# Two neighbouring rows per partition in the expert gate and up weight loads of an encoder trunk, one core

## The reference, cut to what matters

```python
def grouped_moe(h, w_router, router_bias, w_gate, w_up, w_down):
    t = h.reshape(-1, dm)                       # 512 tokens x 1024 in the kernel
    ...                                         # scores, a group of 4 experts, top 2 in it
    out = jnp.zeros_like(t)
    for e in range(N_EXPERTS):                  # 16
        a = jax.nn.silu(t @ w_gate[e]) * (t @ w_up[e])     # (1024, 512) each
        out = out + gate[:, e:e + 1] * (a @ w_down[e])     # (512, 1024)
    return out
```

## Time and profile before

| | |
|---|---|
| median of three runs | 1633.03 us (1631.05 to 1634.56) |
| profiled execution, its own time | 1634.32 us |
| its span, first to last instruction | 1632.7 us |
| TensorE matmul busy | 1432.0 us, 88% |
| VectorE busy | 1010.3 us, 62% |
| ScalarE busy | 874.8 us, 54% |
| granted TensorE clock, mean | 0.951 of full speed |
| bytes moved by DMA | 342.29 MB |

### The profile page before, as it was taken

How to read it: one execution, slowest core, us unless ns; L and a number is a source line. 1 busy time by engine, 2 the same in 40 slices (tenths; PEclk the granted TensorE clock), 3 DMA queues, 4 the chain that set the end, 5 groups by cost and what they waited for, 6 DMA issues and landing times.

```text
span 1632.7 us, 19147 instructions
## 1 busy us (share of the span) xinstructions
PE 1432.0 (88%) x6710; PEld 1083.7 (66%) x6710; DVE 1010.3 (62%) x1258; ACT 874.8 (54%) x1242; POOL 134.6 (8%) x145
## 2 busy tenths in 40 slices
PE   6799989999749999999769989899995699999996
PEld 3577558887537777777537765687772577777774
DVE  1464674324567888888372938633446688878875
ACT  4532585223237777777363328832323577777764
POOL 1000000000010222222000000000000112222210
PEclk9899999999869999999889999999997799999998
DMA  9532571112257999999762136311322799999954
GB/s 331 187 108 98 207 256 54 52 52 103 103 209 268 367 347 334 346 346 340 268 234 103 52 134 245 138 52 53 108 99 103 281 333 349 338 349 345 344 190 159
DMA packets 148654, 342.29 MB, mean 210 GB/s; under 512 B 8430, under 2 KB 10624, under 8 KB 148464
## 3 DMA queue, kind: packets, MB, share of 16 engines
q1 hardware_dynamic: 136880, 317.20, 53.9%
q0 software_dynamic: 10992, 23.43, 3.9%
q10 hardware_dynamic: 720, 0.84, 0.2%
HBM read 334.10 MB, written 24.12 MB: 219 GB/s over the span
## 4 chain that ended last, share of the span: by engine, by line
PE 56%; DMA 15%; DVE 10%; issue 8%; ACT 8%; POOLq 2%; DVEq 0%; PEldq 0%; SPq 0%; ACTq 0%; PEld 0%
PE bank L725 11%; PE bank L727 11%; PE bank L726 11%; DMA y_by_choice<-zone,row_now 7%; DMA zone<-rows_by_token,row_now 5%; PE bank L1068 2%; PE bank L1070 2%; PE bank L1069 2%; DVE w_lo L2149 2%; PE bank L758 2%; POOLq L2282 2%; PE bank L1053 2%; PE bank L1054 2%; PE bank L1055 1%; ACT x_lo L1456 1%
## 5 line engine op out<-in xcount | busy, mean ns | idle before, releaser
L725 PE MATMUL bank<-x_hi,w_lo 128*128 128x512 f32 x608 | 246.0, 405 | 28.1 <-DVE x_lo L1661 17.4
L727 PE MATMUL bank<-x_hi,w_hi 128*128 128x512 f32 x608 | 239.1, 393 | 0.0
L726 PE MATMUL bank<-x_lo,w_hi 128*128 128x512 f32 x608 | 238.7, 393 | 0.0
L2149 DVE TENSOR_TENSOR w_lo<-ring,zone_r 128x2048 fp32r<-128x2048 f32 x92 | 210.4, 2290 | 27.7 <-ACT zone_r L1456 27.7
L1456 ACT CAST x_lo<-ring 128x2048 fp32r<-128x2048 f32 x96 | 184.1, 1920 | 62.6 <-PE bank L1055 26.2
L1456 ACT CAST zone_r<-ring 128x2048 fp32r<-128x2048 f32 x96 | 183.0, 1914 | 24.0 <-PE bank L1070 13.9
L1638 DVE TENSOR_TENSOR w_lo<-ring,w_hi 128x1024 fp32r<-128x1024 f32 x84 | 102.4, 1221 | 98.7 <-ACT w_hi L1211 98.3
L1053 PE MATMUL bank<-w_lo,zone_r 128*128 128x512 f32 x384 | 157.4, 410 | 5.8 <-issue 5.8
L725 PEld LDWEIGHTS bank<-x_hi,w_lo 128*128 128x128 f32 x608 | 114.9, 189 | 65.2 <-issue 26.1
L726 PEld LDWEIGHTS bank<-x_lo,w_hi 128*128 128x128 f32 x608 | 115.4, 190 | 25.4 <-issue 2.4
L727 PEld LDWEIGHTS bank<-x_hi,w_hi 128*128 128x128 f32 x608 | 115.2, 189 | 25.0
(11 more groups left out here) (296 smaller groups left out, 2704.4 us busy)
## 6 DMA issues: line engine op xcount, KB each, us to landing
ring<-in_w_gate SPq DMA_DIRECT2D x32, 2048.0 KB
ring<-in_w_up SPq DMA_DIRECT2D x32, 2048.0 KB, 13.7
ring<-in_w_down SPq DMA_DIRECT2D x32, 2048.0 KB, 8.7
ring<-in_w_ada SPq DMA_DIRECT2D x24, 2048.0 KB, 9.0
ring<-in_w_in SPq DMA_DIRECT2D x16, 2048.0 KB, 8.4
ring<-in_w_out SPq DMA_DIRECT2D x4, 2048.0 KB, 7.8
zone<-y_by_choice SPq DMA_DIRECT2D x8, 1024.0 KB, 8.1
ring<-in_w_branch_a SPq DMA_DIRECT2D x2, 2048.0 KB, 8.4
```

Of the source, the lines that this page charges most:

```text
L725: mm(out, lo, x_first, start=start, stop=False)
L726: mm(out, hi, x_second, start=False, stop=False)
L727: return mm(out, hi, x_first, start=False, stop=stop)
L2149: v.tensor_tensor(w_low[EXPERT_SLOTS[par][k]][:, cols], ring[EXPERT_SLOTS[par][k]][:, cols], part_hi[buf].bitcast(F32), ALU.subtract)\
```

## The change

The gate and up loads read `128 x 4 x 1024` instead of `128 x 8 x 512`: the partition `p` of block `b` takes the two neighbouring weight rows `256b + 2p` and `256b + 2p + 1`, one piece of 4096 bytes. Chunk `c = 2b + j` of a slot now holds rows `256b + 2p + j`. To match, ScalarE's copy of the transposed token rows sets the columns apart: it reads every second element of a PSUM bank and writes runs of 128, so that block `c` of a gathered row holds the same features. The down loads keep their form, written in the same expression.

```diff
@@ first tile's weights of a layer (SyncE)
                 for k, (name, s) in enumerate(zip(("w_gate", "w_up", "w_down"), EXPERT_SLOTS[0])):
                     sp.wait_ge(used[s], layer * SLOT_BLOCKS[s] + SLOT_BLOCKS[s])
-                    sp.dma_start(ring[s][:, :].rearrange("p (k n) -> p k n", k=(KC, KC, FC)[k]),
-                                 t_in[name][layer:layer + 1, 0, :, :].rearrange("o (k p) n -> p (o k) n", p=P))\
+                    j = (2, 2, 1)[k]
+                    sp.dma_start(ring[s][:, :].rearrange("p (b n) -> p b n", b=FC),
+                                 t_in[name][layer:layer + 1, 0, :, :].rearrange("o (b p j) n -> p (o b) (j n)", p=P, j=j))\
                       .then_inc(w_landed[0][k], 16)
@@ load_weights (SyncE)
-                    sp.dma_start(ring[EXPERT_SLOTS[par][k]][:, :].rearrange("p (k n) -> p k n", k=(KC, KC, FC)[k]),
+                    j = (2, 2, 1)[k]
+                    sp.dma_start(ring[EXPERT_SLOTS[par][k]][:, :].rearrange("p (b n) -> p b n", b=FC),
                                  t_in[name][layer:layer + 1, bass.ds(e, 1), :, :]
-                                 .rearrange("o e (k p) n -> p (o e k) n", p=P))\
+                                 .rearrange("o e (b p j) n -> p (o e b) (j n)", p=P, j=j))\
                       .then_inc(w_landed[par][k], 16)
@@ rows by token (ScalarE)
-                        nc.scalar.copy(rows_tok[:, t, half * 512:(half + 1) * 512], ps[:, :])\
+                        nc.scalar.copy(rows_tok[:, t, half * 512:(half + 1) * 512]
+                                       .rearrange("p (b j i) -> p b j i", b=2, j=2),
+                                       ps[:, :].rearrange("p (b i j) -> p b j i", b=2, j=2))\
                             .then_inc(S["rows_ready"], 1)
```

## The result

The kernel after takes **1647.26 us** (median of four runs, 1641.86 to 1651.03), beside 1632.65 us for the kernel before on the same chip: 1.0081 times as long, 95% interval 1.0061 to 1.01. It is slower, where faster was forecast, and outside the range. The profiled execution took 1641.86 us (span 1640.3 us), 7.6 us of span more than the one of before; it is the shortest of the four, so its trace shows only about half of the loss. A second trace of the same kernel, further down, shows the rest.

A forecast was written before the change was run, and what follows sets the result against it. TensorE's wait for the next tile's gather was taken as the bound; 25 waits x 0.7 us, less about 0.5, made 17 us, so 1634.3 became 1617 profiled and 1616 us median. Range for 8 in 10: 1606 to 1644.

The forecast's parts named there:

- What bounds the kernel: Expert stages: TensorE waits for the next tile's gather, late behind scatter and index copy, 25.9 us in 25 waits.
- Packets: Queue q1: 64 gate and up loads go from 1024 to 512 packets, leaving about 104,100.
- What a load costs: DMA engines: each gate or up load 0.55 us cheaper, 1.1 us a tile; a lone `w_up` at 5.5 us.
- What the gather gets: Gather beside `w_up` at a tile's end: latency 0.7 us less, from 7.0 to about 6.3 us.
- The gain: Gather: `w_up`'s data stops about 1.1 us earlier, so the gather loses 0.8 us less to contention.
- The cost: Gather rows standing behind 4096-byte packets: 0.075 us a row, 0.3 to 0.6 us if alternating one for one.
- second rival: Longer packets hold up the gather between 625.5 and 632 us: slower, 1636 to 1655, likeliest 1643 us; chance 0.25.
- The scatter: Beside `w_down`, its end beside `w_gate`: latency unchanged at 7.9 us; slightly earlier landing worthless while VectorE's subtraction holds the index copy.
- The row copies: ScalarE's eight copies a layer, reading PSUM with a step of two: cost 0, with 0 to 3 us for both layers.
- The first gathers: Each layer's first gathers, beside `w_gate`, fully exposed: could move 0.3 us either way, under 1 us in total.
- The sum: Whole kernel: 25 waits x 0.7 us, less about 0.5, makes 17 us less, hence 1616 us.
- the longer half: Upper part of the second rival's slower outcomes, chance 0.12, left out of the 8-in-10 range.

The follow-up runs named there:

- after_again: The kernel after, unchanged, measured once more on another chip: 1646.84 us, 1.0088 times before.
- gate4k: Kernel before with only the `w_gate` load in 4096-byte pieces, row copies as before: 1651.12 us, 1.0107 times before.
- gu8k: Kernel after with four neighbouring rows per partition (8192-byte gate and up packets, row copies with a step of four): 1636.10 us, 1.0024 times before.
- early_after: Kernel after, with GpSimd's code putting the next gather ahead of the wait for the last scatter to land: 1634.34 us, 1.0008 times before.
- up4k: Kernel before with only the `w_up` load in 4096-byte pieces, row copies as before: 1636.36 us, 1.0029 times before.
- early_before: Kernel before, with GpSimd's code putting the next gather ahead of the wait for the last scatter to land: 1613.26 us, 0.9872 times before.

## Why the prediction was wrong

- **What bounds the kernel: right.** The time lay in the chain of scatter, index copy and gather; with it gone the kernel runs in 1605.89 us, where 1607 had been worked out. (The row of 40 slices was read too widely: the digit 9 stands in six slices of each stage, not in eight, and the lowest of them moves 333 GB/s.)
- **Packets: right** (104,112). **What a load costs: right in kind, too large in size.** The lone `w_up` took 5.7 us where 5.5 was forecast, and over the whole run a load became cheaper by 0.40 us, not 0.55, and a tile by 0.8, not 1.1. The Trainium skill (DMA: Bandwidth & Descriptors, Why small descriptors are slow) led to 0.13 us a load, an estimate; the trace shows three times that, so the row was the better guide.
- **What the gather gets: the step that failed.** The forecast was 0.7 us less in every tile; the median is 0.2 us more, and that of the gathers with a fast issue is 7.0 us as before. Both terms were mis-sized. *The gain, 0.8 us:* it spread the gather's 3.8 us of contention evenly over the 5.1 us from its issue to the end of `w_up`. In the packets of before the first row of a gather moves only 4.4 us after the issue, when the backlog is nearly over, and the last 1.8 us later. `w_up` did land 0.9 us sooner, but the first row moves 0.2 us sooner in after (4.2 us), and the end behind the last row is 0.1 us shorter. *The cost:* the sum took 0.1 us, below its own 0.3 to 0.6; the stretch from first row to last grew by 0.4. The 0.1 rested on a pair of rows that was no comparison: the scatter beside `w_ada` and the usual one, taken to stand beside 4096-byte packets, both move their rows beside 2048-byte ones. The second rival had the right direction and, at its low end of one packet a row, the right size; its other end, 3.0 us, with all of the contention counted in packets, is not borne out. The Trainium skill's sentence behind it (DMA: Bandwidth & Descriptors, Queues, rings and completion order), that an engine changes queues only at packet boundaries, agrees in direction with the scatter and the first gathers from 2048 bytes on. But the packet of that page holds several descriptors, 9 to 17 as a rule, and is not the single piece that the profile counts, so it gives no price for the length of a piece.
- **The scatter, forecast unchanged: wrong,** 8.7 us instead of 7.9, because its rows move beside `w_gate`, whose packets grew. The cover was read right but is thin: the scatter landed some 0.3 us ahead of the subtraction that holds the index copy. A scatter 0.8 us later pushes the gather out 13 us and more after the tile's start in some tiles, and beside the next subtractions, where its issue takes up to 3.1 us and it lands after 8.3. No step had the issue of the gather as a cost. That it is the longer issue which makes the gather late is read from the rows of all runs and was not tried by itself.
- **The row copies: right.** With a step of two they last as before, and the last store of rows goes out at 460.31 us, 14 us ahead of the first gather at 474.47:

```profile
454.27 0.59 ACT L1445 COPY zone<-bank 128x512 f32<-128x512 f32 x1
...
455.25 4.77 ACT L1445 COPY zone<-bank 128x512 f32<-128x512 f32 x7 [0.39 <-ACT zone L1445]
...
460.31 0.53 POOL L2264 DMA_DIRECT2D rows_by_token<-zone  x1 [0.17 <-issue]
```

- **The first gathers: "0.3 us either way" was too little,** 2.1 us of waiting in all.
- **The sum.** 17 us less became 5.0 + 2.1 us more. No step had TensorE's clock either, which fell with most waits of 2 to 3 us; how much of each dip came out as time is not shown. The second rival's likeliest price, 1643 us, lacks both: the median is 4 us over it.
- **The numbers.** The rival had 0.25 and its range reached 1644, leaving out "the longer half": the result lies 3 us beyond. A mechanism with a priced upper end of 3.0 us a gather deserved more of the range than one pair of rows could take from it.

## What to carry to other kernels

A cheaper load is worth what the one who waits gets from it. Here the engine time saved was real and the waiting transfer, in another queue, still lost, because at 4096 bytes the longer packets in its way cost it more than the shorter backlog gives; so ask first which packets move in the very stretch in which the awaited transfer's own packets move. The load that it is issued beside need not be the one. Where two small indirect DMAs stand one behind the other on a tile's path, putting them side by side with their indices ready before both is worth far more (26.7 us here) than any packet size. It leaves 4.6 us of the 14.6 that the change cost, though the DMA engines then become the next limit, and all loads in 2048-byte packets cost 8.5 us. Look at the lengths of TensorE's waits, not only at their sum, and at how long the issue of an indirect DMA takes.

## What the runs showed of the hardware that was not expected

- Short waits cost TensorE its clock. In the expert stages of after, after_again, gate4k, gu8k and early_after it waited 21 times for a gather for 1.84 to 3.35 us; with 17 of these the clock stood at 1.2 GHz for some 3.4 us (in two of them twice as long), 1.7 us at full speed missing. With none of the 36 waits of 1.27 to 1.75 us in these and in up4k did it fall, and the trace of before has none over 1.24 us.
- The latency of an indirect DMA beside plain loads rises with the loads' packets from 2048 to 8192 bytes (scatter 7.9, 8.7, 9.4 us), and hardly from 1024 to 2048 (7.6, 7.9). It is the stretch in which the rows move that grows (2.7, 3.2, 3.9 us); the 4.5 us ahead of the first row stay.
- GpSimd, with an index copy and a `drain` behind an indirect DMA, did not go on until that DMA had landed (8.1 us in early_before), though the program waits for no semaphore of it there. Whether it is the drain or something else of GpSimd's queue was not tried by itself.
- The issue of a gather on GpSimd took 2.15 to 3.15 us instead of 1.03 in 15 of gate4k's 28, each with one of VectorE's subtractions of 128 by 2048 beside it for at least 1.2 us; these landed after 8.2 us, the others after 7.05 (medians). Where it began just ahead of a subtraction (526.48 and 526.50 us in before) it was not held.
- ScalarE's copy out of PSUM with a step of two floats costs nothing measurable: 0.59 us as before.
